# A two-model transformer kernel in split fp32r: another order of matmuls in a tile, gates from split weights, a third chunk in one prepass, another prologue

## The reference, cut to what matters

```python
# first block, layer l (hybrid_layer)
h = rms_norm(x, attn_pre_gain)
u = h @ w_in                       # 4120 columns: q, k, v of two attentions,
                                   # 24 columns g_nsa, 2 x 1024 columns g_a, g_b
gates = sigmoid(g_nsa)             # of the sparse attention's three branches
...                                # sliding window and sparse attention, with rope
mixed = sigmoid(g_a) * (o_a @ w_branch_a) + sigmoid(g_b) * (o_b @ w_branch_b)
x = x + rms_norm(mixed @ w_out, attn_post_gain)
h = rms_norm(x, ffn_pre_gain)
c = causal_conv3(h @ ffn_w_up)     # 2 x 2816 columns
x = x + rms_norm((gelu(c[:2816]) * c[2816:]) @ ffn_w_down, ffn_post_gain)

# second block, layer l
f = swiglu(rms_norm(x, g0), gate, up, down);  x = x + 0.5 * rms_norm(f, g1)
m = mixer(rms_norm(x, g2));                   x = x + rms_norm(m, g3)
f = swiglu(rms_norm(x, g4), gate, up, down);  x = x + 0.5 * rms_norm(f, g5)
```

## Time and profile before

| | before |
|---|---|
| median of 3 runs | 1836.9 us (1836.74 to 1837.92) |
| profiled execution | 1835.49 us, its span 1833.6 us |
| PE busy | 1770.3 us (97%), 9874 matmuls |
| PE weight loads busy | 1498.3 us (82%) |
| DVE busy | 1224.4 us (67%) |
| ACT busy | 1052.6 us (57%) |
| POOL busy | 661.7 us (36%) |
| DMA | 307.22 MB, mean 168 GB/s |
| mean granted PE clock | 0.984 of 2.4 GHz |

### The profile page before, as it was taken

How to read it: one execution, slowest core, us unless ns; L and a number is a source line. 1 busy time by engine, 2 the same in 40 slices (tenths; PEclk the granted TensorE clock), 3 DMA queues, 4 the chain that set the end, 5 groups by cost and what they waited for, 6 DMA issues and landing times.

```text
span 1833.6 us, 26407 instructions
## 1 busy us (share of the span) xinstructions
PE 1770.3 (97%) x9874; PEld 1498.3 (82%) x9874; DVE 1224.4 (67%) x1924; ACT 1052.6 (57%) x1988; POOL 661.7 (36%) x656
## 2 busy tenths in 40 slices
PE   5989999999989999999999999999999999999998
PEld 5865888888865888888888887888888888778887
DVE  6855689975765689976665644766476657356663
ACT  5567576665477576655555556655465536565543
POOL 3114316620113326622662012566046600306640
PEclk9979999999989999999999999999999999899999
DMA  8731566665631566675766561765666575327661
GB/s 233 194 99 29 179 171 191 176 222 169 159 109 46 162 184 184 176 234 164 203 177 218 172 196 47 205 186 180 210 184 184 173 240 189 111 70 207 188 210 72
DMA packets 412224, 307.22 MB, mean 168 GB/s; under 512 B 10083, under 2 KB 366773, under 8 KB 412097
## 3 DMA queue, kind: packets, MB, share of 16 engines
q1 hardware_dynamic: 411312, 304.82, 56.5%
q0 software_dynamic: 784, 0.72, 0.2%
HBM read 304.45 MB, written 1.05 MB: 167 GB/s over the span
## 4 chain that ended last, share of the span: by engine, by line
PE 94%; ACT 3%; DVE 2%; issue 1%; DMA 1%; SPq 0%; POOL 0%; DVEq 0%; ACTq 0%
PE bank L1295 34%; PE bank L1296 17%; PE bank L1367 8%; PE bank L1368 8%; PE bank L1369 8%; PE bank L1345 3%; PE bank L1346 3%; PE bank L1335 3%; PE bank L1511 2%; PE bank L1493 1%; PE bank L1482 1%; DMA raw<-in_w_in 1%; ACT whi L511 1%; PE bank L1568 1%; ACT hsA L511 1%
## 5 line engine op out<-in xcount | busy, mean ns | idle before, releaser
L1295 PE MATMUL bank<-hsA,whi 128*128 128x512 f32 x2496 | 891.9, 402 | 2.1 <-DVE TA L823 2.1
L815 DVE TENSOR_TENSOR wlo<-raw,whi 128x1024 fp32r<-128x1024 f32 (+1 forms) x568 | 726.4, 1304 | 201.9 <-ACT whi L511 198.1
L1296 PE MATMUL bank<-hsA,wlo 128*128 128x256 f32 x2496 | 703.5, 282 | 0.0
L511 ACT ACTIVATE whi<-raw 128x1024 fp32r<-128x1024 f32 (+1 forms) x568 | 571.1, 1033 | 132.1 <-PE bank L1369 98.2
L1295 PEld LDWEIGHTS bank<-hsA,whi 128*128 128x128 f32 x2496 | 472.6, 189 | 120.0 <-DVE wlo L815 3.2
L1296 PEld LDWEIGHTS bank<-hsA,wlo 128*128 128x128 f32 x2496 | 474.8, 190 | 0.2
L511 ACT ACTIVATE low<-bank 128x256 f32<-128x256 f32 (+1 forms) x404 | 151.0, 377 | 367.9 <-PE bank L1296 330.4
L1179 POOL TENSOR_TENSOR HB<-CB,UB 128x256 f32<-128x256 f32 x88 | 123.7, 1406 | 363.7 <-ACT CB L514 363.1
L1367 PE MATMUL bank<-whi,hid 128*128 128x512 f32 x528 | 206.0, 390 | 0.0
L1369 PE MATMUL bank<-wlo,hid 128*128 128x512 f32 x528 | 205.6, 389 | 0.0
L1368 PE MATMUL bank<-whi,hid 128*128 128x512 f32 x528 | 205.4, 389 | 0.0
(11 more groups left out here) (217 smaller groups left out, 2014.2 us busy)
## 6 DMA issues: line engine op xcount, KB each, us to landing
raw<-in_ffn_w_up SPq DMA_DIRECT2D x176, 512.0 KB, 5.2
raw<-in_ffn_w_down SPq DMA_DIRECT2D x120, 512.0 KB, 4.5
raw<-in_w_in SPq DMA_DIRECT2D x104, 512.0 KB, 5.9
raw<-in_ffn_w_gate SPq DMA_DIRECT2D x88, 512.0 KB, 4.0
raw<-in_w_out SPq DMA_DIRECT2D x32, 512.0 KB, 4.5
raw<-in_ffn_w_down SPq DMA_DIRECT2D x24, 256.0 KB, 3.0
G<-in_norm_g SPq DMA_DIRECT2D x12, 512.0 KB, 7.5
raw<-in_cmp_w SPq DMA_DIRECT2D x8, 512.0 KB, 5.3
```

What stands on the lines that cost most here:

```text
L511: return nc.scalar.activation(out_, in_, func, **kw)
L815: v.tensor_tensor(wlo[c_ % RING][:, x:y], raw[:, c_ % RAW, x:y], whi[c_ % RING][:, x:y].bitcast(F32), ALU.subtract)\
L1295: mm(bank[b][:, 0:2 * n], whi[slot][:, at:at + P], rhs[:, 0:2 * n], start=x == 0, stop=False, **g32)
L1296: ins = mm(bank[b][:, n:2 * n], wlo[slot][:, at:at + P], rhs[:, 0:n], start=False, stop=x == len(ks) - 1, **g32)
```

## The change

1. In a tile the two matmuls of every odd row block change places: H L, L H, H L, L H, so that equal ones stand beside each other.
2. The gates of the first block are no longer computed from an unsplit copy of the rows. `wg` is split into a high and a low part (`wgs`, 48 columns), 8 matmuls of 512 columns run over `hsA` after the fifth chunk, ACT copies the result out of PSUM (`GS`), and four small matmuls with a constant (`pair`) add the parts after the next chunk. The copies `Y` are gone.
3. Norm 2 has three chunks in its prepass, as the others have.
4. The prologue: x's first half is loaded first, of the constants only the identity before the panels and the rest behind the second panel; both halves' squares are taken before the first split; the angles are computed on POOL ahead of its small loads. Where DVE had a combined multiply-add, POOL has two instructions.
5. Small consequences: other PSUM banks for the rope and value transposes, a few more waits.

```diff
-    THREE = [n not in (0, 2) for n in range(LAST)]
+    THREE = [n != 0 for n in range(LAST)]
...
+        sp.dma_start(X[:, 0, :], a["x"][0, 0:P, :]).then_inc(x_in[0], 16)
         sp.dma_start(posi[:, :], a["positions"][0:1, :].broadcast_to([P, S])).then_inc(consts_in, 16)
         sp.dma_start(const[:, at:], a["const"][:, at:]).then_inc(consts_in, 16)
-        for th in range(2):
-            sp.dma_start(X[:, th, :], a["x"][0, th * P:(th + 1) * P, :]).then_inc(x_in[th], 16)
         gain_pre(0)
-        sp.dma_start(const[:, 0:at], a["const"][:, 0:at]).then_inc(ident_in, 16)
+        sp.dma_start(const[:, 0:P], a["const"][:, 0:P]).then_inc(ident_in, 16)
+        sp.dma_start(X[:, 1, :], a["x"][0, P:2 * P, :]).then_inc(x_in[1], 16)
         for L, p in enumerate(PLAN.one):
             n = 2 * L
             for s, (c, _) in enumerate(p["in"]):
                 panel(c, a["w_in"][L], s * 256)
+                if c == 1:
+                    sp.dma_start(const[:, P:at], a["const"][:, P:at]).then_inc(masks_in, 16)
...
-        norm(0, 0, keep=True)
+        for th in range(2):
+            act.wait_ge(x_in[th], 16)
+            for dh in range(2):
+                square(X[:, th, half(dh)], th, 4 + dh)
+            rsqrt(0, th, 1, 1.0)
+        high(0, 0)
+        split_to(1)
+        high(0, 1)
         act.wait_ge(angles_ready, 1)
         f(sinT[:, :], ang[:, 3, :], ACT.Sin)
         f(cosT[:, :], ang[:, 4, :], ACT.Sin).then_inc(tables_ready, 1)
...
-                if c == 1:
+                if c == 2 and L == 0:
+                    act.wait_ge(wg_in, 16 * DEPTH)
+                    f(wgs[:, :, :, 0:24], wg[:, :, :, :], ACT.Copy).then_inc(wg_hi, 1)
+                if c == 4:
+                    act.wait_ge(gates_part, L + 1)
+                    f(GS[:, :], bank[4][0:48, :], ACT.Copy).then_inc(gates_copied, 1)
+                if c == 6:
                     act.wait_ge(gates_sum, L + 1)
...
-        norm(0, 0)
+        for th in range(2):
+            dve.wait_ge(x_in[th], 16)
+            scaled(0, th)
+        for th in range(2):
+            lower(0, th)
+            split_to(th)
+        dve.wait_ge(masks_in, 16)
         dve.wait_ge(tables_ready, 1)
...
+        pool.wait_ge(consts_in, 32)
+
+        seq.link(g_.tensor_copy(ang[:, 0, :], posi[:, :]))
+        seq.link(g_.tensor_scalar(ang[:, 0, :], ang[:, 0, :], C("freq"), 1.0, ALU.mult, ALU.mult))
+        for n, turn in ((3, 0.0), (4, 0.25)):
+            k, r, t = ang[:, 1, :], ang[:, n, :], ang[:, 2, :]
+            seq.link(g_.tensor_scalar(k, ang[:, 0, :], 1.0 / TWO_PI, turn, ALU.mult, ALU.add))
+            seq.link(g_.tensor_scalar(k, k, ROUND, 0.0, ALU.add, ALU.add))
+            seq.link(g_.tensor_scalar(k, k, ROUND, 0.0, ALU.subtract, ALU.add))
+            rest = ang[:, 0, :]
+            for part in (PI_A, PI_B, PI_C):
+                seq.link(g_.tensor_scalar(t, k, -part, 1.0, ALU.mult, ALU.mult))
+                seq.link(g_.tensor_tensor(r, t, rest, ALU.add))
+                rest = r
+            seq.link(g_.tensor_scalar(r, r, turn * TWO_PI, PI_MAX, ALU.add, ALU.min))
+            ins = g_.tensor_scalar(r, r, -PI_MAX, 1.0, ALU.max, ALU.mult)
+            if n == 3:
+                seq.link(ins)
+        ins.then_inc(angles_ready, 1)
         pool.wait_ge(cleared, 2)
...
             for x, (at, rhs) in enumerate(ks):
-                mm(bank[b][:, 0:2 * n], whi[slot][:, at:at + P], rhs[:, 0:2 * n], start=x == 0, stop=False, **g32)
-                ins = mm(bank[b][:, n:2 * n], wlo[slot][:, at:at + P], rhs[:, 0:n], start=False, stop=x == len(ks) - 1, **g32)
...
+                if x % 2:
+                    lower()
+                    ins = high()
+                else:
+                    high()
+                    ins = lower()
             ins.then_inc(sum_ready, 1)
...
+                if c == 4:
+                    pe.wait_ge(wg_split, 1)
+                    pe.wait_ge(params_ready, 1)
+                    for k in range(KD):
+                        ins = mm(bank[4][0:48, :], wgs[:, L, k, :], hsA[:, k, :], start=k == 0, stop=k == KD - 1, **g32)
+                    ins.then_inc(gates_part, 1)
+                if c == 5:
+                    pe.wait_ge(gates_copied, L + 1)
                     for b in range(2):
-                        for k in range(KD):
-                            ins = mm(bank[4][:, 24 * b:24 * b + 24], Y[:, k, b * P:(b + 1) * P], wg[:, L, k, :],
-                                     start=k == 0, stop=k == KD - 1, **g32)
+                        g_ = bank[4][:, 24 * b:24 * b + 24]
+                        mm(g_, GS[:, b * P:(b + 1) * P], C("pair")[0:48, :], start=True, stop=False, **g32)
+                        ins = mm(g_, GS[0:24, S + b * P:S + (b + 1) * P], C("pair")[0:24, :], start=False, stop=True, **g32)
                     ins.then_inc(gates_sum, 1)
```

More of the change, by code:

```diff
@@ L555, in rsqrt, with norm @@
             f(ns[:, th, k + 3:k + 4], ns[:, th, k + 3:k + 4], ACT.Exp, scale=-0.5).then_inc(r_ready, 1)
-        def norm(n, next_c, keep=False):
+        def norm(n, next_c):
             for th in range(2):
[L560 to L567, removed]
+                act.wait_ge(pass_done, STAGES[n - 1]["last"][th])
+                square(y_bank(th, 1)[:, :], th, 1)
+                rsqrt(n, th, 0, FACTOR[n])
+                if th:
+                    split_to(next_c + 1)
                 if n == LAST:
@@ L848, in norm @@
             for th in range(2):
[L849 to L858 removed]
+                dve.wait_ge(ss_ready, ss_at(n, th, 1))
@@ L863, in norm @@
-                dve.wait_ge(g2_in, 16 * n + 16)
-                if n:
-                    dve.wait_ge(x_ready, x_at(n, th, 1))
-                for dh in range(2):
-                    v.scalar_tensor_tensor(H[:, th, half(dh)], X[:, th, half(dh)], ns[:, th, 7:8], G2[:, half(dh)],
-                                           ALU.mult, ALU.mult).then_inc(h_ready, 1)
-                if n and th == 0 and STAGES[n - 1]["late"]:
-                    first_gains(n, (1,))
-                if n == 0 or th == 0:
-                    split_to(next_c + th)
@@ L873, in norm @@
[L873 to L880 removed]
+                dve.wait_ge(x_ready, x_at(n, th, 1))
@@ new lines, in norm, with scaled @@
+                scaled(n, th)
+                if th == 0 and STAGES[n - 1]["late"]:
+                    first_gains(n, (1,))
+                if th == 0:
+                    split_to(next_c)
+                lower(n, th)
+            if n < LAST:
+                split_to(next_c + 1)
+        def scaled(n, th):
+            bias(n, th, 1, 1.0)
+            dve.wait_ge(r_ready, r_at(n, th, 1))
+            dve.wait_ge(g2_in, 16 * n + 16)
+            for dh in range(2):
+                v.scalar_tensor_tensor(H[:, th, half(dh)], X[:, th, half(dh)], ns[:, th, 7:8], G2[:, half(dh)],
+                                       ALU.mult, ALU.mult).then_inc(h_ready, 1)
@@ L882, in token_major, with lower @@
+        def lower(n, th):
+            for dh in range(2):
+                dve.wait_ge(hi_ready, h_at(n, th, dh))
+                hi = hsA[:, 4 * dh:4 * dh + 4, th * P:th * P + P]
+                v.tensor_tensor(hsA[:, 4 * dh:4 * dh + 4, S + th * P:S + th * P + P],
+                                y_bank(th, dh)[:, :].rearrange("p (k t) -> p k t", t=P), hi.bitcast(F32), ALU.subtract)\
+                    .then_inc(hs_ready, 1)
         def token_major(n):
```

113 lines of the change are left out of this document (48 added, 65 removed).

## The result

| | before | after |
|---|---|---|
| median (lowest to highest) | 1836.74 us (1832.79 to 1837.92, 5 runs) | 1822.42 us (1818.9 to 1824.65, 5 runs) |
| ratio, 95% interval | | 0.9926 [0.9911, 0.9941] |
| profiled execution, span | 1835.49, 1833.6 us | 1822.42, 1820.6 us |
| mean granted PE clock | 0.984 | 0.987 |

Forecast were 1817.1 us and a range of 1807 to 1833. The time is inside the range, 5 us above the point. The parts of the sum are another matter: the order gave about what was forecast, for partly other reasons, a fall of the clock that is absent gave 3.8 us that nobody had foreseen, and the other parts gave almost nothing.

A forecast was written before the change was run, and what follows sets the result against it. TensorE was taken as the bound, with 94% of the chain that ended last. Order -8.3, layer 0 -6.4 and layer 1 -5.1 sum to -19.8 us: from 1836.9 to 1817.1 us, range 1807 to 1833.

The forecast's parts named there:

- order: Chunk tiles: H L L H halves the changes of matmul size, saving 3.3 ns on each of 2496 pairs, -8.3 us.
- layer 0 without the order: Prologue and gates of layer 0: earlier start, chunk 2 9.1 us earlier, gates +2.7; sum -6.4 us (-10 to -1).
- layer 1 without the order: Layer 1: gates -0.8, norm 2's stops -1.7, chunk +0.1, clock fall -2.7; sum -5.1 us (-7 to -1).
- B: Tiles: like neighbours remove all of the mixing price, another -8.3 us less some DVE waits; 1809.3 us, 20%.
- C: Tiles: the new order changes nothing; 1825.4 us, 15%.
- E: Tiles: every change from low to high costs 30 ns; slower, 1846.2 us, 7%.
- Prologue up to the second pass: Layer 0: chunk 0 lands at 12.8, PE starts at about 15.1, 6.3 us earlier; transposes 20.7, second pass from 22.8.
- 5 to 20, hidden: Layer 0: angles on POOL take 13 us plus links, about 5 to 20; ACT asks at about 23, so no cost.
- rival D: Prologue: angles late on POOL, chain ends at 36 to 39, ACT stands 13 to 16 us; 1832.1 us, 8%.
- The gates: Each layer of block one: 8 matmuls of 512 columns and 4 small float32 ones, 2.7 us against 3.49 before.
- The stop: Norm 2, layer 1: a third prepass chunk removes 1.16 us idle and turns 1.57 into 1.07, -1.7 us.
- The -2.7 for the clock: Layer 1 behind norm 2: the 6.8 us fall to half clock disappears, 28 matmuls taking 3.4 instead of 6.02 us.

The follow-up runs named there:

- runs of four: Changed kernel with each tile's matmuls as four high halves, four low, then four low, four high; 1821.87 us, ratio 0.9935.
- e1_order_alone: The kernel before with only the new order of matmuls in a tile (H L L H); 1822.15 us, ratio 0.9932.

## Why the prediction was right, and where it was not

Set against the 13.0 us between the two spans. The order's part is the trace of the order alone against the kernel before, without the clock in the last mixer; the layers' parts are the changed kernel against the order alone. Layer 0's start varies by 3 us between kernels that are alike there, so its row is rough.

| term | forecast | from the traces |
|---|---|---|
| order | -8.3 | about -9.0 |
| layer 0 without the order | -6.4 | -0.4 |
| layer 1 without the order | -5.1 | 0.0 |
| clock in the last mixer | not in it | -3.8 |

- **Order: the size came out by luck.** I had 3.3 ns on all 2496 pairs. Measured were 5.0 ns, but not on all of them: block two's tiles lost 7.1 us (1440 pairs) and the up-projections 2.6, the in-projection of layer 1 only 0.5 and that of layer 0 some 1.2, because alternation ran at 346.7 ns in part of them. And 2.5 us came back in the down-projections. I had charged nothing there and named 1.2 us for each of two layers as the upper bound; the upper bound is what happened. At equal clock the order is worth 7.1 to 7.4 us; the difference to 9.0 is open. That the time follows from H L L H is shown by undoing it; that it hangs on the number of changes of size is refuted by runs of four, and the premise that mixing as such costs 6.7 ns a pair by the in-projections.
- **Rivals B, C and E** fall by the pair alone: 348.3 ns, where they needed 346.7, 353.3, or 358. That the order changes nothing is refuted by `e1_order_alone` as well. The Trainium skill, "TensorE: Matmul & The Clock Gate", section "Back-to-back issue gap", gives N/2.4 + 2.5 ns for an isolated matmul and says that in a real kernel weight loads and matmuls together set the spacing. The trace agrees that the formula is not enough here: 512 columns take 226.7 ns where it gives 215.8.
- **Prologue up to the second pass: right.** Landing and split at 14.03 (forecast 12.8), start 16.08 (15.1), second pass 23.92 (22.8).
- **The failed step is "5 to 20, hidden".** The angles ran from 6.2 to 27.8, past the 23 us from which rival D decides. I had summed 13.0 us of instructions at 478 and 726 ns; they took 19.6, and the links between them 2.0. Nearly all of the excess lies in eight of them, the constant added and subtracted and the two bounds: 10.3 us where I had 3.8. They are slow by themselves. In the seven kernels with the angles on POOL the adding and the subtracting took 1.07 to 1.10 us each time that no DVE instruction ran beside them, as at 18.27 and 19.44 above, where a multiplication took 0.40 to 0.41. With every operation at the shortest seen, the chain is still 19.3 us and ends at 25.5. What runs beside it, DVE above all, adds about 2.3 us; the longest single instruction took 1.93. So the row of 478 ns was that of another operation. D named the right wait, its reason is the smaller part of the delay, and its price was too high (2.98 us on ACT, not 13 to 16). Giving the angles back to DVE, with the small loads earlier, returns 4.5 us at equal clock, 5.5 in the trace; how much of it is the angles and how much the loads is not separated.
- **The gates** cost 3.17 us a layer instead of 2.7 against 3.49 before. Timeline of PE:

```profile
58.02 2.02 PE L1449 MATMUL bank<-hsA,wgs 128*48 128x512 f32 x8
59.88 0.81 PE L1472 MATMUL bank<-U,const 128*128 128x256 f32 x3
...
66.42 0.40 PE L1455 MATMUL bank<-const,GS 48*128 48x24 f32 x2
...
67.73 0.48 PE L1472 MATMUL bank<-U,const 128*128 128x256 f32 x1
```

  The eight take 1.86 us as forecast; the four small ones 1.31 us, 0.33 each and not 0.22.
- **Layer 1.** The stop went as forecast (2.73 us of idle time became 1.07), and yet the layer has nothing of the -5.1 left. Three things ate it. The first rope matmuls now wait for DVE: the 22 of the layer hold PE 5.06 us instead of 4.08, and 4.09 in the kernel with two chunks. The scores, transposes and products of attention took 1.4 us more (56.7 instead of 55.3). And the half clock lasts 3.4 us longer in sum. The -2.7 for the clock was the wrong step: I priced the fall that I saw and not the ones that follow when it is avoided.
- The clock gave back in block two what no row before foretold. Without it the change would have come out near 1826. The point was missed by 5 us because gains and losses that I had not foreseen were of like size.

## What to carry to other kernels

Price an operation moved to GpSimd by rows of the same arithmetic on GpSimd, with VectorE busy beside it, and bring every DMA issue behind it into the sum: here a hidden chain of 13 us became 21.6 and took nearly the whole gain of the prologue. Read a price in every stage in which it will be charged: the alternation cost 6.7 ns a pair in one stage and nothing in another. If an engine is at 100% in a stage, what another engine wins there is a loan, and its next wait calls it in. When differences of less than 0.5% matter, compare runs at the same mean clock, and never book the end of one fall of the clock as a gain before a run has shown that no other takes its place.

## What the runs showed of the hardware

- Matmuls of 512 and 256 columns in turn had two rates under one order: strict alternation took 353.3 ns a pair in the up-projections and block two, and in the first block's in-projections partly 346.7. In pairs it was 348.3 everywhere, in runs of four 349.2.
- A matmul of 256 columns took 120 ns behind another in a run of four, and 113.5 to 117 directly behind one of 512.
- A DVE step with three inputs of 256 columns takes 470 ns, or 950 to 967 while a GpSimd product of two inputs runs.
- GpSimd's scalar operation on 256 columns depends on its arithmetic: 0.40 to 0.41 us for two multiplications, 1.07 to 1.10 for two additions or a subtraction and an addition, both with VectorE idle; beside VectorE up to 0.95 for the first, and up to 1.93 for the addition with an upper bound.
- A fp32 matmul of 24 columns over 48 or 24 rows costs 0.33 us for each one written, in two records.
- Falls of the granted clock to 0.50 lasted 3.4, 6.8, 10.2 or 13.7 us, most of them in the attention of block one, and shifted by changes hundreds of microseconds away.
